# A two-layer encoder in two token halves: experts of one half placed between the trunk instructions of the next

## The reference

```python
for l in range(DEPTH):                                   # DEPTH = 2
    mod = cond @ w_ada[l] + b_ada[l]                     # six modulation vectors
    h = _rms(x, g_norm_mix[l]) * (1.0 + sc_m) + sh_m
    gq, gk, gv, galr, gr, qc, kvc, ik, iw, prw, gates = _split(h @ w_in[l], IN_SIZES)
    y_a = _gla(...)      # chunked gated linear attention
    y_b = _dsa(...)      # each query keeps its top 128 keys, softmax over them
    y_c = _rwkv7(...)    # delta-rule state update over time
    merged = g_a * (y_a @ w_branch[l, 0]) + g_b * (y_b @ w_branch[l, 1]) + g_c * (y_c @ w_branch[l, 2])
    x = x + gt_m * (merged @ w_out[l])
    h2 = _rms(x, g_norm_ffn[l]) * (1.0 + sc_f) + sh_f
    x = x + gt_f * _peer(h2, ...)
return _rms(x, g_final)

def _peer(...):          # for every token: 8 heads, 16 experts each
    s1, i1 = lax.top_k(s[:, :, 0], 16); s2, i2 = lax.top_k(s[:, :, 1], 16)
    top_s, pos = lax.top_k(s1 + s2 (all 256 pairs), 16)
    e_idx = ...; gate = softmax(top_s)
    act = gelu(u[e_idx] . x)                             # one row of u per expert
    return sum over the 128 experts of gate * act * v[e_idx]
```

## Time and profile before

| | |
|---|---|
| time, 3 runs | median 4964.72 us (4957.39 to 4975.81) |
| span of the profiled execution | 4948.7 us; only its span is recorded, its own time is taken as the median, 16.0 us more |
| instructions | 47208 |
| busy share of the span | PE 84%, DVE 48%, ACT 30%, POOL 37% |
| DMA queue of the gathers | 1073.81 MB, 54.0% of the DMA engines' span |
| DMA queue of SP (weights) | 147.10 MB, 8.5% |
| mean granted PE clock | 0.944 of full speed |

### The profile page before, as it was taken

The page is one execution under the profiler, slowest core; times in us unless marked ns, Lnnn a source line. Parts: engine busy times, 40 slices in busy tenths (PEclk is TensorE's granted clock), DMA queues, the critical chain, the costliest instruction groups (busy, mean ns, idle before and its releaser), DMA issues.

```text
span 4948.7 us, 47208 instructions
## 1 busy us (share of the span) xinstructions
PE 4132.8 (84%) x13124; PEld 1989.5 (40%) x13124; DVE 2398.6 (48%) x5272; ACT 1495.9 (30%) x4212; POOL 1841.8 (37%) x2164
## 2 busy tenths in 40 slices
PE   7999999987777777787789999999877877777776
PEld 3587444453332232232236864454532332323222
DVE  1442235156656656654424421451566566566444
ACT  2212222123333333333322223130233333333333
POOL 0121000005666666666501210000066666666664
PEclk9999999998989999999999999999999999999999
DMA  7200111128999999999962001112299999999997
GB/s 245 93 1 1 56 51 64 60 97 349 409 381 399 389 398 391 394 404 404 387 220 69 1 18 39 64 52 71 94 375 410 389 403 388 398 403 390 405 418 311
DMA packets 223816, 1223.93 MB, mean 247 GB/s; under 512 B 18240, under 2 KB 59840, under 8 KB 89024
## 3 DMA queue, kind: packets, MB, share of 16 engines
q0 software_dynamic: 147456, 1073.81, 54.0%
q1 hardware_dynamic: 76096, 147.10, 8.5%
HBM read 1218.74 MB, written 2.10 MB: 247 GB/s over the span
## 4 chain that ended last, share of the span: by engine, by line
PE 31%; POOL 22%; issue 19%; DVE 9%; DMA 8%; PEld 4%; ACT 3%; DVEq 1%; PEldq 1%; POOLq 1%; ACTq 0%; SPq 0%
POOL reg L1781 15%; DMA reg<-uv,e_ic 7%; POOL e_ic L1778 7%; PE bank L914 5%; PE bank L459 5%; PE bank L593 3%; PE bank L504 3%; PEld bank L459 3%; PE bank L847 2%; PE bank L584 2%; DVE reg L1700 2%; DVE reg L1613 2%; PEld bank L775 1%; DVE reg L1608 1%; PE bank L675 1%
## 5 line engine op out<-in xcount | busy, mean ns | idle before, releaser
L914 PE MATMUL bank<-reg,hT 128*128 128x512 f32 x4096 | 2027.3, 639 | 602.7 <-ACT hT L1240 602.4
L1700 DVE CUSTOM_DVE_ANT_0 reg<-reg 128x1024 f32<-128x1024 f32 x1024 | 1256.5, 1227 | 1031.3 <-DMA reg<-uv,e_ic 957.1
L1781 POOL DMA_INDIRECT reg<-uv,e_ic x1024 | 1206.0, 1178 | 855.0 <-POOL e_ic L1778 748.9
L914 PEld LDWEIGHTS bank<-reg,hT 128*128 128x128 f32 x4096 | 777.5, 201 | 1849.8 <-ACT hT L1240 1076.2
L1778 POOL COPY e_ic<-e_idx 128x1 uint32<-128x1 uint32 x1024 | 494.8, 483 | 1456.5 <-DVEq L1678 1286.6
L1234 ACT ACTIVATE reg<-reg 128x1 f32<-128x1 f32 x1024 | 207.2, 202 | 1488.4 <-DVEq L1701 1487.5
L459 PE MATMUL bank<-hT,reg 128*128 128x512 f32 x1120 | 497.1, 598 | 8.2 <-issue 6.2
L1240 ACT ACTIVATE hT<-con,reg 128x128 f32<-128x128 f32 x1024 | 411.1, 401 | 75.2 <-issue 5.6
L1759 POOL TENSOR_TENSOR reg<-reg,con 128x512 f32<-128x512 f32 x112 | 140.8, 1270 | 751.2 <-DVEq L1412 496.6
L459 PEld LDWEIGHTS bank<-hT,reg 128*128 128x128 f32 x1120 | 211.9, 191 | 283.4 <-issue 283.4
L1236 ACT ACTIVATE reg<-reg 128x1 f32<-128x1 f32 x1024 | 301.5, 294 | 72.9 <-issue 3.1
(11 more groups left out here) (260 smaller groups left out, 3396.6 us busy)
## 6 DMA issues: line engine op xcount, KB each, us to landing
reg<-w_ada SPq DMA_DIRECT2D x36, 1024.0 KB, 6.7
reg<-w_mac SPq DMA_DIRECT2D x16, 1536.0 KB, 6.5
reg<-w_in SPq DMA_DIRECT2D x10, 2048.0 KB, 9.4
reg<-uv,e_ic POOLq DMA_INDIRECT x1024, 8.5
reg<-w_ada SPq DMA_DIRECT2D x6, 2048.0 KB, 10.6
reg<-w_mb SPq DMA_DIRECT2D x8, 1536.0 KB, 6.5
reg<-w_out SPq DMA_DIRECT2D x4, 2048.0 KB, 7.9
reg<-w_pq SPq DMA_DIRECT2D x4, 2048.0 KB, 7.8
```

Source lines behind the costliest of these rows:

```text
L914: last = mm(acc[j][:, :], e_diag[:, s_, :], e_row[s_][:, D + j * NB:D + (j + 1) * NB], start=False, stop=False)
L1700: V.tensor_tensor_reduce(e_row[s_][:, 0:D], e_row[s_][:, 0:D], e_hc, 1.0, 0.0, ALU.mult, ALU.add, e_dot[:, s_:s_ + 1])
L1781: pool.indirect_dma_start(e_row[s_], None, uv, bass.IndirectOffsetOnAxis(ap=e_ic[:, s_:s_ + 1], axis=0))\
```

## The change

The 512 tokens are cut into two halves of 256. The program is now four *laps*: layer 0 half 0, layer 0 half 1, layer 1 half 0, layer 1 half 1. Each lap runs the whole trunk for its 256 tokens and routes the first 64 slots of its first tile. The experts of a lap (256 slots: 2 tiles x 128) are placed between the trunk instructions of the next lap; the experts of the last lap stand alone at the end. Recurrent state, keys and latents are kept for the second half (`r_state`, `r_raw`, `g_carry`, `d_kv`, `d_ik`, `d_kt`), and all trunk products have 256 columns.

A fixed table sets the order. `lap_plan` walks over the names of all PSUM results of a lap and gives each an opening and a filling time on a planned clock, in units of about a microsecond. `Turns` deals out the 256 slots evenly along that clock; each engine calls `turns.upto(...)` before it opens or reads a result, and the slots that are due stand there. `Turns` gives every engine a lag in slots: DVE 0, ACT 0.3, PE 1.5, POOL 4 slots early.

```diff
-    for half, t, q, stage in rwkv_steps():        (layer_banks, TILE_BANKS: eight banks, a fixed list)
+PACE = dict(head=2.0, prep=4.0, scan=1.35, gla=1.0, dsa=1.0, mac=1.0, att=1.5, mb=1.0, out=1.0, pq=1.0)
+COST = 3.5
+ROUTE_US, ROUTE_PIECES = 9.0, 8
+class Turns:
+    def __init__(self, steps=None, lag=0.0, plan=None):
+        self.steps, self.i = steps, 0
+        self.pace = plan.total / (N_SLOT + 2) if plan else 0.0
+        self.lag = lag * self.pace
+    def upto(self, at):
+        while self.steps is not None and self.i * self.pace + self.lag <= at:
+            self.step()
```

The experts change too. The row buffers are six (`RING = 6`), of their own memory. The index copy on POOL goes; the DMA reads `e_idx` itself. Some slots are summed on DVE instead of PE: the first 8 and the last 4 of each tile, and from slot 70 of a lap on two of every five (93 of the 256 slots of each of the first three laps, 24 of the last):

```diff
+def on_dve(e, j):
+    s = j % SLOTS
+    if s < HEAD_DVE or s >= SLOTS - TAIL_DVE:
+        return True
+    return e < LAPS - 1 and j >= DVE_FROM and j % 5 in (1, 3)
...
+                    if j % SLOTS == 0:
+                        V.tensor_scalar(e_acc[:], v, w, None, ALU.mult).then_inc(dve_rows, 1)
+                    else:
+                        V.scalar_tensor_tensor(out=e_acc[:], in0=v, scalar=w, in1=e_acc[:], op0=ALU.mult, op1=ALU.add).then_inc(dve_rows, 1)
...
+                for j in range(N_SLOT):
+                    ...
+                    for t_, hh, i in PIECES.get(j, ()):
+                        piece(i, e, t_, hh)
+                    ...
+                    dve.wait_ge(rows_landed[r], 16 * (n // RING + 1))
+                    V.tensor_tensor_reduce(row[r][:, 0:D], row[r][:, 0:D], e_h[t][:], 1.0, 0.0, ALU.mult, ALU.add, e_dot[:, r:r + 1])
+                    dve.drain().then_inc(dots, 1)
+                    if s:
+                        weighted(j - 1)
```

More of the change, by code:

```diff
@@ L103, in rwkv_steps @@
+BLOCK_N = {(lap,) + b: n for n, (lap, b) in enumerate((lap, b) for lap in range(LAPS) for b in lap_blocks(lap % 2))}
 def rwkv_steps():
[L107 removed]
+    units = [(t, q) for t in range(TH) for q in range(2)]
     for step in range(5 * (len(units) - 1) + 10):
@@ L150, in layer_banks @@
-    o += [("h2", t, h) for t in range(TT) for h in range(2)]
-    return o
-TILE_BANKS = [("sc", p, q) for q in range(2) for p in range(2)] + [("acc", 0), ("acc", 1), ("xt", 0), ("xt", 1)]
-def trunk(nc, fixed, cols, consts, x_t, w_ada, w_in, w_small, w_uq, w_iq, w_mac, w_mb, w_out, w_pq, uv, out,
-          depth=L):
+            names = ([("s", t, q)] if t < TH - 1 or h == 0 else []) if half else [("y", t, 0, q), ("y", t, 1, q)]
+        for n in names:
+            p.one(n, 0.8)
+    p.pace = PACE["gla"]
@@ new lines, in lap_plan @@
+    p.pace = PACE["out"]
+    p.group([("wo", m) for m in range(4)], COST)
+    p.one(("ss", 1), 0.5)
+    p.group([("wo", m) for m in range(4, KD)], COST)
+    p.now += 4.0
+    p.pace = PACE["pq"]
+    p.group([("pq", x) for x in range(4)], COST)
+    for k in range(2):
+        p.one(("sc", 0, k, 0), 1.0)
+    for x in range(2):
+        p.one(("h2", 0, x), 0.5)
+    p.group([("pq", x) for x in range(4, EH)], COST)
+    for t, q in ((0, 1), (1, 0), (1, 1)):
+        for k in range(2):
+            p.one(("sc", t, k, q), 1.0)
@@ new lines, in lap_plan, with lap_rows, __init__, bank @@
+    p.routing = p.now
+    p.now += ROUTE_US * ROUTE_PIECES
+    p.total = p.now
+    for x in range(2):
+        p.one(("h2", 1, x), 0.5)
+    return p
+def lap_rows(h):
+    return [b for b in range(TH * h, TH * h + TH) if b > 0]
+PLANS = [lap_plan(lap % 2) for lap in range(LAPS)]
+class Banks:
+    def __init__(self, sem, prefix, order, size):
+        self.n = {name: i for i, name in enumerate(order)}
+        assert len(self.n) == len(order)
+        self.size = size
+        self.filled_sems = [sem(f"{prefix}_filled{b}") for b in range(size)]
+        self.freed_sems = [sem(f"{prefix}_freed{b}") for b in range(size)]
+    def bank(self, name):
+        return self.n[name] % self.size
+    def turn(self, name):
+        return self.n[name] // self.size
+    def filled(self, name):
+        return self.filled_sems[self.bank(name)]
+    def freed(self, name):
+        return self.freed_sems[self.bank(name)]
@@ new lines, with step, rest @@
+class Turns:
[6 more added lines that the diff above has]
+            self.step()
+    def step(self):
+        self.i += 1
+        if next(self.steps, None) is None:
+            self.steps = None
+    def rest(self):
+        while self.steps is not None:
+            self.step()
@@ L159, in trunk @@
+def trunk(nc, fixed, cols, consts, x_t, w_ada, w_in, w_small, w_uq, w_iq, w_mac, w_mb, w_out, w_pq, uv, out):
     ctx = ExitStack()
@@ new lines, in _ @@
+                need("h_ready", 2 * KD)
+                columns("pq", [(("pq", x), x * P, P, 0) for x in range(4)], 512, (0,))
+                keys = block_place((lap, "key"))[0]
+                arrive("key")
+                score(0, 0)
+                h2_rows(0)
+                columns("pq", [(("pq", 4 + x), x * P, P, 0) for x in range(4)], 512, (1,))
+                for t, q in ((0, 1), (1, 0), (1, 1)):
+                    score(t, q)
+                pe.drain().then_inc(used("key"), 1)
@@ L942, in _, with final_sum @@
+                turns.rest()
+                h2_rows(1)
+            def final_sum(h):
+                pe.wait_ge(end_squares, h + 1)
+                for k in range(KD):
+                    last = mm(psum[h][:, 0:SH], ones, fin[h][:, k, :], start=(k == 0), stop=(k == KD - 1))
+                last.then_inc(end_sum, 1)
+            final_sum(0)
+            Turns(expert_steps(LAPS - 1)).rest()
+            final_sum(1)
         @block.scalar
```

2362 lines of the change are left out of this document (1204 added, 1158 removed).

## The result

| | |
|---|---|
| kernel before, 4 runs | median 4961.76 us |
| kernel after, 4 runs | median 4824.77 us (4816.17 to 4826.75) |
| ratio, 95% interval | 0.9723 [0.9707, 0.974] |
| forecast | 4500 us (4050 to 4900) |
| span of the profiled execution | 4814.4 us, mean granted PE clock 0.891 (before 0.944) |

The account below looks back on a forecast made before the run. Trunks were taken as limited by PE (1107 us a layer) and experts by DMA (1359 us), in series. Laps of 627 + 2 x 1019 + 1073 + 745 = 4483 us, with 16 added 4499, gave 4500; range 4050 to 4900.

Parts of the forecast that it names:

- the step that failed: Prep, lap with half 1: largest of DVE 240, DMA 218 and PE 191 us, so 240, set by DVE.
- The eight stages after the scan: Middle laps, gla to pq and routing: sums of 518 us (half 1) and 486 (half 0), with 8% 559 and 525.
- 8% "for waits in turn": Middle laps, stages after the scan: 8% added to their sums, 518 to 559 us with half 1.
- The scan: Middle laps: 8.2 us a step x 25 = 205 us with 42 slots, 198 with 38; 143 without slots.
- the 0.7 that I let show: Scan: of the slots' 3.6 us of DVE work a step, 0.7 of it lengthens the step, giving 8.2 us.
- the two rules: Skill page's DVE lock on GpSimd (34 us a lap, forecast 4600) and 1380 ns table-load drain (about 4520), weighed against the trace.
- First lap: Trunk without experts: half of 1107.1 us, plus 20, 12, 14 and 27 for parts not halved, together 627 us.
- That leaves 451: Whole kernel: 1973 us saved on experts, less 1449 for three longer middle laps and 73 for the first, leaves 451.
- Waits in turn cost much more: Rival, middle laps: scan 278 us (265 in the other lap), later stages 20% over their sums, total 4896; chance 0.18.
- The ring of six is too small: Rival, row buffers: slot's way of 28 us cancels the gain, 30 us gives 5230 total; chance 0.08.
- The stages even out: Rival, middle laps: work carries across stage borders, a lap costs its largest whole sum, total about 4050; chance 0.14.
- The other signs: Profile after: DVE above 85% in second lap's prep, DMA near 0.95 in third's, PE some 80% in scan, 380 table loads.

Follow-up runs that it names:

- prep27: Kernel after with the planner's weight of prep 2.7 in place of 4.0, so fewer slots stand in prep: 4758.62 us, 0.9607 of the kernel before.
- mix21: Kernel after with prep weight 2.0, scan 1.45, routing units 14 slots apart, TensorE 2.5 slots behind, three of five sums on VectorE from slot 46: 4736.63 us, 0.9553.

## Why the forecast was 331 us short

In the span, laps of 657, 1141, 1158, 1124 and 734 us against the forecast's: +30, +122, +85, +105, -11.

**Prep: the step that failed, +147 us (55, 41 and 51).** "Prep, 75 slots: DVE ... = 240; DMA ... = 218; PE ... = 191. So 240, DVE" takes the largest of three sums over the whole stage. I had written that six buffers can't carry work from stage to stage, and did not apply it inside a stage. The bound changes within prep. Four stretches of the second lap's prep (the second, the fourth and the last two eighths):

```profile
720.10:756.90 36.80, 29.22 (x78) 15.31 (x77) 30.69 (x86) 17.10 (x45) 14.06 (x12) 0.94 0.86 308
793.70:830.50 36.80, 26.68 (x59) 11.90 (x59) 27.69 (x58) 24.68 (x43) 9.07 (x7) 0.82 0.70 257
904.10:941.00 36.90, 30.88 (x90) 16.49 (x89) 15.78 (x27) 14.59 (x43) 14.48 (x13) 1.00 1.00 397
941.00:977.80 36.80, 19.60 (x47) 9.45 (x45) 23.96 (x37) 23.25 (x42) 10.47 (x9) 0.76 0.77 293
```

With routing pieces DVE is 75 to 90% busy and the transfers have gaps; past the pieces the transfers are at 1.00 and DVE at 43%; at the end a chain of small steps crosses engines. So one stage has at least three limits in turn, and none of the three sums is its time. The chain at the end shows in the timelines of ScalarE and VectorE:

```profile
953.74 1.28 ACT L1082 ACT_TABLE_LOAD   x1
955.03 0.47 ACT L1082 ACTIVATE reg<-bank,sc 128x256 f32<-128x256 f32 x1
955.52 1.28 ACT L1039 ACT_TABLE_LOAD   x1
956.82 0.20 ACT L1039 ACTIVATE e_ge<-e_dot 128x1 f32<-128x1 f32 x1
...
957.87 1.28 ACT L1082 ACT_TABLE_LOAD   x1
...
961.00 1.33 ACT L1085 ACTIVATE reg<-reg 128x256 f32<-128x256 f32 x4
```
```profile
961.45 1.43 DVE L1606 TENSOR_TENSOR reg<-reg 128x256 f32<-128x256 f32 x4 [6.46 <-ACT reg L1085]
```

A 0.20 us gelu between two 0.47 us activations brings two loads of 1.28 us, and DVE stands 6.46 us; its next dots stand behind it. Shown by the runs, for the second lap: VectorE's work (-27 us of prep when halved), the number of slots there (prep27, -53 for 19 slots), ScalarE's loads (-15), TensorE's work nearly nothing (-5 for 30 us less). The third lap's prep, 341 us, is another case: its transfers are at 0.91, that is 311 us where I had 300, and the halved dot took only 11 us off it. How the 55 us of the second lap divide between the three limits was not tried.

**The eight stages after the scan, +135 us (52, 32 and 51).** Mb (62) and routing (77 to 80) came as forecast, gla below. Dsa with mac (232 against 184) and att (73 against 57) did not: 24 us of the first are the halved trunk's own (152 against 128), the rest the slots, whose DVE, ACT and PE steps stand in turn among small dependent steps. In the second lap the halved dot took 15 us off, the copy for gelu 11, the halved sums 3 and all at once 32; how the remaining 49 over the stage alone divide is open. The 8% "for waits in turn" was the term that was too small. The largest sum, PE's, was taken as the bound; in the trace PE is busy 81 to 84% there.

**The scan, +21 us in three laps.** 209 to 210 us against 205 and 198. That it came near is in part luck, two errors that offset each other: alone it takes 134 us where I had 143, and the slots add 75 where I had 62. VectorE's slot work in it is 92 us in the trace, of which the 75 are 0.8 and not the 0.7 that I let show; halving the dot showed 0.67 of what it took away. Some of the 92 is waiting for GpSimd's masks, see the two rules below.

**First lap +30, heads +10, last lap -11.** In the first lap no slot runs; its prep took 122 us where half and the modulation give 77 + 12 = 89, and its dsa and mac 148 where halves give 128; the scan took 8 less than I had. Why prep does not halve there was not tried.

**The account of the gain.** "That leaves 451" stands 15 under the forecast's own difference (4948.7 to 4483), because it counts the two layers of the kernel before (2 x 2466) and not the 17 us that follow them. The forecast does not rest on it.

**The rivals.** "Waits in turn cost much more" (laps of 1155, 1198 and 1155 in their order, 4896 us) came nearest: laps of 1141, 1158 and 1124. But the scan was not its place, and a longer lag of TensorE gave only 33 us; work in turn, mostly VectorE's, is the better name. "The ring of six is too small" is refuted as what holds the middle laps (+9, +20 and +2 with five; a larger ring was not tried) and holds for the last lap, whose round trip I had put at 2.3 us a slot: with five rows it cost 51 us. "The stages even out" did not come.

**The other signs.** DMA carried 1314.92 MB (forecast 1.32 GB), the loads are 380 of 1.283 us as forecast, PE is 91% busy in mac (109.42 of 120.10 us). DVE's share of prep was to be above 85% and was 74%: by my own list that was the sign against the step. Of the other signs, the transfers of the third lap's prep were at 0.91 (0.95) and PE at 84% in the scan (80). A sum on DVE took 1.33 us (taken 1.4).

**The two rules weighed.** GpSimd's masks hardly grew, 1286 ns on average against 1270, but the lock is there, and it is VectorE that waits. The first mask of the second lap's scan and the dot that meets it:

```profile
981.60 1.26 POOL L1889 TENSOR_TENSOR reg<-reg,con 128x512 f32<-128x512 f32 x1 [9.51 <-DVEq L1643]
```
```profile
981.69 2.26 DVE L1480 CUSTOM_DVE_ANT_0 row<-row,e_h 128x1024 f32<-128x1024 f32 x1 [0.29 <-issue]
```

The dot takes 2.26 us where 1.22 is usual, and ends 1.08 us after the mask. In the three scans 49 dots and 7 sums on VectorE overlap a mask, and together they last 50 us longer than as many of them elsewhere (1.225 and 1.285 us): 19, 14 and 17 us a lap, where the forecast's 4600 took 34 on GpSimd. With nothing interleaved no dot takes over 1.35 us. How much of it shows in the scan's time was not tried. A gather's issue took 1219 ns on average, 1020 with halved dots.

A load is followed by its activation after 0.01 us, and starts 0.02 us after the one before it (rows above: 955.50 to 955.52), so the drain that the Trainium skill gives in "ScalarE: Activation LUTs", What ACT_TABLE_LOAD costs, is in none of these rows; a switch cost 1.28 us.

## What to carry over

When two streams share engines in a fixed order, do not take the largest engine sum of a stage. In stages that are chains of small dependent steps, lay the guest's work on the engine that both use end to end with the stage's own time (here that gave 283, 220, 245 and 78 us for stages that took 295, 209, 232 and 73, and halving a part of it showed about two thirds of what it took away); only where one engine or the transfers are over 90% busy is its sum near the answer. First run the halves with nothing interleaved: the price per slot and stage that this gives (3.0 in prep, 0.4 to 1.2 in gla, mb and out) says where to put the guest's work, and moving it by that table gave 66 us at once. The prices hold for the first slots moved and not for every lap: in the third lap the move gave 2 us, and the last step (mix21) cost 46.
